# The convolution branch's pointwise projection in three rounded products, beside attention

## The chip, the cores and the metric

The kernel runs on one core of one Trainium2 chip. The metric is the device time of one execution, in microseconds (us), lowest to highest over three runs with their median. Inside a core, TensorE (PE) multiplies matrices, with its weight loads shown apart as PEld; VectorE (DVE), ScalarE (ACT) and GpSimd (POOL) do the elementwise work; SyncE (SP) issues most DMAs. Each engine works through its own instructions in their order and waits for the others on semaphores.

## What is computed

Two transformer-like blocks on 256 tokens of width 1024. The change lies in the first block, in the branch that runs beside attention:

```python
def conformer_conv(u, conv_w, conv_b, ln_g, ln_b, w_pw):
    a, g = jnp.split(u, 2, axis=-1)
    y = a * jax.nn.sigmoid(g)
    y = lax.conv_general_dilated(y, conv_w[:, None, :], ...) + conv_b
    y = jax.nn.silu(layer_norm(y, ln_g, ln_b))
    return y @ w_pw

def merge_branches(u, attn_heads, ...):
    y_a = attn_heads.reshape(b, n, N_HEADS * V_DIM) @ w_o_mla
    y_c = conformer_conv(...)
    g = jax.nn.sigmoid(u[..., OFF_GATE:])
    return (g[..., :D_MODEL] * y_a + g[..., D_MODEL:] * y_c) @ w_out
```

Attention has 16 heads, 256 queries and 512 keys. After it come a retrieval layer that gathers 256 pairs of rows per token lane by index, and a second block with a routed mixture of experts.

## The kernel before

**Layout.** Activations lie with features on the partitions: `convz` is the normed convolution output, [128, 8, 256], eight slices k of 128 features. Weights come through three ring buffers of 2 MB each (`ring`), loaded by SP in the order of `STREAM`; a load waits until `w_used` says that the buffer's former block was taken up.

**Two ways to multiply.** A float32 matmul of 128x256 stands in the trace as two records. Where a product is made "in three", weight and activation are each cut in a rounded high part (type fp32r) and the rest: ACT copies 1024 columns of weights to a `hi` buffer (`weight_round`, L1484; the ACT helper is L1416 in the trace), POOL subtracts it from the ring in place (L1938, the `lo` part), and PE adds hi x hi, hi x lo (L775) and lo x hi (L780), one record each. Before the change this is done for the input projection (28 weight tiles), the attention output projection `w_o` (8 tiles) and `w_out` (6). The weight tiles are numbered in one sequence, c; ACT may round tile c once the rounded products of tile c-3 are issued (`split_done`), since there are three `hi` buffers.

**Attention stage.** 32 units n (16 heads, two halves of the queries). PE's order is written out by `attention_order`: scores S(n+2) (L684), transposes T(n) of unit n's probabilities (L869), after every fourth unit a head pair's output O (L899), and some steps C of the convolution projection (L884). A step C is one output slice m and one input slice k, float32, accumulating in `psY`; there are 64 steps, 6 in unit 0, then one or two a unit. DVE works for unit n: row maximum of S(n) (L2115), bias (L2116), then reciprocal (L2120) and scaling by 1/sum (L2121) of unit n-1, head outputs (L2099, L2100), and after every 16 steps C the gate multiplication (L2108). ACT does exp(n) with its row sum, then the eviction of T(n-1). So T(n) needs L2121 of unit n, which in DVE's queue stands behind the row maximum of S(n+1).

**Just before attention** eight groups q, k, v are projected; DVE evicts q (L2082 to L2087), ACT k and v, and in groups 4 to 7 ACT also applies SiLU to two slices of `convz` each. Then DVE sums the modulation (L2094, L2095). POOL has nothing to do from 183 us until unit 30, where the rounding of `w_o` begins.

Of the kernel before, what the change touches and what calls it, by code (L numbers as in the profile page):

```python
# [20 lines left out]
F32 = mybir.dt.float32  # L21
# [24 lines left out]
SPLIT_IN, SPLIT_O, SPLIT_OUT = 28, 8, 6  # L46
AT_O = SPLIT_IN
# [113 lines left out]
def split_block(c):  # L161

    if c < SPLIT_IN:
        return first_block(2 + 2 * (c // 4)), c % 4
    c -= SPLIT_IN
    for name, n, skip in (("w_o", SPLIT_O, 0), ("w_out", SPLIT_OUT, 2)):
        if c < n:
            return STREAM[name] + (c + skip) // 4, (c + skip) % 4  # L170
        c -= n
# [105 lines left out]
def build(nc, w, out):  # L277
# [3 lines left out]
    with ExitStack() as ctx:  # L281
# [13 lines left out]
        def rounded(*places):  # L295
# [21 lines left out]
        attn_hi, attn_lo, merged_hi, merged_lo = rounded(  # L317
            ("attn_hi", 4096, K, T), ("attn_lo", 6144, K, T), ("merged_hi", 18432, K, T), ("merged_lo", 20480, K, T))
# [54 lines left out]
        convz = ar(12288, K, T)  # L373
        qT, kT, V = ar(14336, HEADS, T), ar(18432, HEADS, 2 * T), ar(26624, 4, D)
# [36 lines left out]
        def split_hi(c):  # L411
            return (hi1_a, hi1_b, hi1_c)[c % 3] if c < SPLIT_IN else top_hi[c % 3]
# [252 lines left out]
        def _(pe):  # L665
# [190 lines left out]
            for kind, n in order:  # L856
# [7 lines left out]
                elif kind == "T":  # L864
                    pe.wait_ge(p_ready, n + 1)
                    if n >= 2:
                        pe.wait_ge(pt_copied, n - 1)
                    for j in range(4):
                        last = nc.tensor.transpose(aux(2 + n % 2)[:, j * P:(j + 1) * P],  # L869
                                                   Pb[:, n % 2, j * P:(j + 1) * P], ident)  # L870
                        if n + j == 0:
                            last.then_inc(w_used, 2)
                    last.then_inc(pt_ready, 1)
                elif kind == "C":


                    m, k = divmod(n, K)
                    if n == 0:
                        pe.wait_ge(conv_out, K)
                        pe.wait_ge(stat_used, STATS.index("var") + 1)  # L880
                    if m >= 4 and m % 2 == 0 and k == 0:
                        pe.wait_ge(conv_gated, m // 2 - 1)
                    wt = use(STREAM["w_pw"] + m // 4) if k == 0 and m % 4 == 0 else wt
                    last = nc.tensor.matmul(aux(m // 2 % 2)[:, (m % 2) * T:(m % 2 + 1) * T],  # L884
                                            wt[:, k * 512 + (m % 4) * P:k * 512 + (m % 4 + 1) * P], convz[:, k, :],
                                            start=(k == 0), stop=(k == K - 1))
                    if m == 4 and k == 0:
                        last.then_inc(w_used, 1)
                    if m % 2 and k == K - 1:
                        last.then_inc(conv_proj, 1)  # L890
                else:

                    ps = tile(ATT[kind, n])
                    pe.wait_ge(tile_free["act"], readers[:TILE["v7"] + 1].count("act"))
                    pe.wait_ge(pt_copied, 4 * n + 4)
                    for j in range(4):
                        for h in (2 * n, 2 * n + 1):
                            lo = VD * (h % 2)
                            last = nc.tensor.matmul(ps[lo:lo + VD, 0:T], V[:, j, h * VD:(h + 1) * VD], PT[:, h % 4, j, :],  # L899
                                                    start=(j == 0), stop=(j == 3))  # L900
                    last.then_inc(tile_ready, 1)
# [210 lines left out]
            def second_pair(i, n):  # L1112

                ps = tile(i)
                if n in (0, 6):
                    pe.wait_ge(h_split, 2 * K)
                    pe.wait_ge(h_hi_ready, 2 * K + (n > 0))
# [288 lines left out]
        def _(act):  # L1406
# [132 lines left out]
            for m in range(8):  # L1539
# [5 lines left out]
                if m == 2:  # L1545
                    root()
                if m >= 4:
                    act.wait_ge(convn_ready, 1)
                    for k in (2 * m - 8, 2 * m - 7):
                        fn(convz[:, k, :], convz[:, k, :], ACT.Silu, scale=vcol("ln_g", k),  # L1550
                           bias=vcol("ln_b", k)).then_inc(conv_out, 1)
            fn(warm, ones[:, 0:1], ACT.Exp)

# [9 lines left out]
            for n in range(n_units + 1):  # L1563
                if n < n_units:
# [7 lines left out]
                    act.sem_inc(tile_free["act"], 1)  # L1572
                if n:
# [328 lines left out]
        def _(pool):  # L1902
# [26 lines left out]
            for c in range(SPLITS):  # L1929
                if c == SPLIT_IN:  # L1930
# [5 lines left out]
                    pool.wait_ge(kr_spread, 2)  # L1936
                pool.wait_ge(u_hi_ready, c + 1)
# [16 lines left out]
            for k in range(K):  # L1954
                pool.wait_ge(h_hi_ready, K + k + 1)
# [12 lines left out]
        def _(dve):  # L1968
# [107 lines left out]

            tab = {lo: rope_tab[lo:lo + 32, :].rearrange("p (a t) -> p a t", a=1).broadcast_to([32, 2, T])
                   for lo in (64, 96)}
            for m in range(8):
# [10 lines left out]
                if m == 3:  # L2090
                    dve.wait_ge(convc_ready, 1)
                    tt(convz, convz, over(rstd(5), K), ALU.mult).then_inc(convn_ready, 1)
            dve.wait_ge(tile_free["act"], readers[:TILE["mod2_3"] + 2].count("act"))
# [18 lines left out]
            for n in range(n_units + 1):  # L2112
                if n < n_units:
                    ps = take(ATT["S", n])
                    seq(nc.vector.tensor_reduce(row_max[:, n:n + 1], ps[:, :], AX.X, ALU.max))  # L2115
                    ts(row_bias[:, n:n + 1], row_max[:, n:n + 1], -ATTN_SCALE, None, ALU.mult).then_inc(nbias, 1)  # L2116
                if n:
# [682 lines left out]
def pack(i):  # L2800
# [21 lines left out]
    for e in range(NEXP):  # L2822
# [17 lines left out]
        "w_pw": cols(a("w_pw")[0]),  # L2840
# [35 lines left out]
```

## Time and profile before

| | |
|---|---|
| median of three runs (lowest, highest) | 1516.78 us (1515.97, 1517.38) |
| the profiled execution: its own time | 1518.48 us |
| its span in the trace | 1516.3 us |
| busy in the span: PE, PEld, DVE, ACT, POOL | 1267.8, 723.6, 876.7, 553.3, 463.0 us |
| mean granted clock of TensorE | 0.885 of full speed |
| attention stage | about 221 to 310 us from the start |
| retrieval stage, gathers by DMA | about 380 to 1045 us |

The trace is of one execution; its span leaves out some 2 us that lie around it in the execution's own time. Busy times of PE are modelled ends of pipelined matmuls: the pitch from one record's start to the next is what a matmul takes of the engine. Line numbers in rows are those of the kernel before.

### The profile page before, as it was taken

The numbers are of one execution on the slowest core, as the hardware profiler recorded it, in microseconds if no ns is written. First come the engines' busy times: TensorE is split into PE (matmuls) and PEld (weight loads), VectorE is DVE, ScalarE is ACT, GpSimd is POOL, SyncE is SP. The second block draws the span as 40 slices with busy tenths as digits, with TensorE's granted clock in tenths as the row PEclk, the third lists the DMA queues.
The fourth block names the chain that finished last, engine by engine and source line by source line (L and its number), as shares of the span: only waits on it lengthen the run. The fifth ranks groups of instructions, "written<-read, shape, count | busy, mean of one in ns | idle before, by whom it ended". The sixth has DMA issues, their size and how long they took to land.

```text
span 1516.3 us, 19635 instructions
## 1 busy us (share of the span) xinstructions
PE 1267.8 (84%) x7450; PEld 723.6 (48%) x7450; DVE 876.7 (58%) x2110; ACT 553.3 (36%) x1107; POOL 463.0 (31%) x374
## 2 busy tenths in 40 slices
PE   7999999999787666666766776677999999999997
PEld 3888766689543111111111312113878987554543
DVE  2799786654598888864555654445647552222112
ACT  2244364532343333332333222224785523212122
POOL 0546600073333333333333332330526413000000
PEclk9999999999999667767677887767999999999999
DMA  9466612145999999999999999999333348899996
GB/s 373 196 254 255 248 66 95 56 177 223 404 370 396 422 415 422 412 421 421 421 421 417 421 421 422 420 421 373 112 111 112 112 183 346 333 428 427 427 427 257
DMA packets 53806, 479.14 MB, mean 316 GB/s; under 512 B 6353, under 2 KB 6737, under 8 KB 8145
## 3 DMA queue, kind: packets, MB, share of 16 engines
q0 software_dynamic: 36864, 268.45, 42.9%
q1 hardware_dynamic: 15552, 206.99, 34.0%
q10 hardware_dynamic: 1296, 2.45, 0.4%
q8 instruction: 59, 0.97, 0.3%
q14 instruction: 35, 0.28, 0.0%
HBM read 476.82 MB, written 1.05 MB: 315 GB/s over the span
## 4 chain that ended last, share of the span: by engine, by line
PE 51%; DMA 29%; DVE 11%; ACT 4%; issue 3%; POOL 1%; SPq 0%; DVEq 0%; ACTq 0%; POOLq 0%
DMA arena<-in_uv,pick 24%; PE psD L684 13%; PE psD L775 7%; PE psD L1303 6%; PE psY L953 5%; DVE arena L2220 5%; PE psD L780 4%; PE psD L1312 3%; ACT arena L1416 3%; DMA arena<-in_experts 2%; PE psY L884 2%; DMA ring<-in_w_in 2%; PE psY L1253 1%; DMA ring<-in_w_mod 1%; PE psY L684 1%
## 5 line engine op out<-in xcount | busy, mean ns | idle before, releaser
L953 PE MATMUL psY<-arena 64*64 64x512 f32 x2048 | 379.4, 835 | 199.9 <-ACT arena L1416 196.1
L1926 POOL DMA_INDIRECT arena<-in_uv,pick x256 | 240.0, 938 | 419.5 <-PE psY L953 400.8
L953 PEld LDWEIGHTS psY<-arena 64*64 64x64 f32 x2048 | 67.7, 163 | 485.4 <-ACT arena L1416 458.2
L2220 DVE CUSTOM_DVE_ANT_0 arena<-arena,psD 128x1024 f32<-128x1024 f32 x128 | 156.3, 1221 | 155.4 <-DMA arena<-in_uv,pick 152.3
L1416 ACT ACTIVATE arena<-arena,pick 128x64 f32<-128x64 f32 x256 | 88.8, 347 | 391.6 <-DVE pick L2220 369.4
L2220 DVE CUSTOM_DVE_ANT_0 arena<-arena,psY 128x1024 f32<-128x1024 f32 x128 | 154.5, 1215 | 56.4 <-DMA arena<-in_uv,pick 55.9
L1416 ACT ACTIVATE arena<-psD 64x512 f32<-64x512 f32 (+4 forms) x128 | 67.5, 533 | 272.8 <-PE psD L1303 105.5
L1416 ACT ACTIVATE arena<-arena 128x64 f32<-128x64 f32 (+4 forms) x301 | 116.3, 387 | 24.5 <-DVE arena L2636 4.6
L2050 DVE SCALAR_TENSOR_TENSOR psY<-arena,pick,psY 128x256 f32<-128x256 f32 x224 | 89.2, 482 | 0.0
L684 PE MATMUL psD<-arena 128*128 128x128 f32 (+3 forms) x420 | 84.5, 345 | 3.7 <-DVEq L2661 2.6
L1416 ACT ACT_TABLE_LOAD x60 | 77.0, 1283 | 8.0 <-DVE pick L2220 5.8
L684 PEld LDWEIGHTS psD<-arena 128*128 128x128 f32 (+2 forms) x420 | 58.4, 202 | 23.0 <-issue 15.3
L2732 DVE TENSOR_TENSOR yrow_lo<-psD,yrow_hi 64x512 fp32r<-64x512 f32 x32 | 22.0, 689 | 70.9 <-ACT yrow_hi L1416 70.4
L1938 POOL TENSOR_TENSOR ring_r<-ring,work_r 128x1024 fp32r<-128x1024 f32 x9 | 22.8, 2546 | 131.1 <-ACT work_r L1416 131.1
L684 PE MATMUL psD<-arena,ring 128*128 128x256 f32 (+1 forms) x240 | 57.5, 395 | 3.3 <-issue 2.7
L1416 ACT ACTIVATE arena<-psY 128x512 f32<-128x512 f32 (+1 forms) x51 | 30.4, 595 | 68.5 <-PE psY L869 35.7
L684 PEld LDWEIGHTS psD<-arena,ring 128*128 128x128 f32 x240 | 45.3, 190 | 12.6 <-issue 5.9
L910 PE MATMUL psD<-xh,ring 128*128 128x256 f32 x192 | 47.2, 392 | 0.0
L910 PEld LDWEIGHTS psD<-xh,ring 128*128 128x128 f32 x192 | 35.5, 193 | 16.2 <-issue 12.2
L2725 DVE SCALAR_TENSOR_TENSOR arena<-psD,arena 64x512 f32<-64x512 f32 x16 | 12.1, 756 | 48.0 <-ACT arena L1416 47.8
L1303 PE MATMUL psD<-arena,xh 128*64 128x512 f32 x160 | 36.5, 594 | 1.1 <-DMA arena<-in_experts 1.1
L1303 PE MATMUL psD<-arena,work 128*64 128x512 f32 x160 | 36.6, 594 | 0.7 <-ACT work L1416 0.7
(441 smaller groups left out, 2373.0 us busy)
## 6 DMA issues: line engine op xcount, KB each, us to landing
arena<-in_experts SPq DMA_DIRECT2D x30, 2048.0 KB, 19.7
ring<-in_w_in SPq DMA_DIRECT2D x18, 2048.0 KB, 9.4
ring<-in_experts SPq DMA_DIRECT2D x18, 2048.0 KB, 17.5
ring<-in_w_mod SPq DMA_DIRECT2D x12, 2048.0 KB, 9.0
ring<-in_w_pq SPq DMA_DIRECT2D x4, 2048.0 KB, 8.2
ring<-in_w_out SPq DMA_DIRECT2D x3, 2048.0 KB, 8.4
ring<-in_w_pw SPq DMA_DIRECT2D x2, 2048.0 KB, 8.2
ring<-in_w_o SPq DMA_DIRECT2D x2, 2048.0 KB, 10.7
```

The source lines that it names most:

```text
L684: last = nc.tensor.matmul(dst, a, b, start=(i == 0), stop=(i == len(pairs) - 1))
L775: last = nc.tensor.matmul(ps, hi[:, k * P:(k + 1) * P], x[:, k, :], start=(k + i == 0), stop=False)
L780: last = nc.tensor.matmul(ps, lo[:, k * P:(k + 1) * P], x_hi[:, k, :], start=False, stop=(k == K - 1))
L884: last = nc.tensor.matmul(aux(m // 2 % 2)[:, (m % 2) * T:(m % 2 + 1) * T], wt[:, k * 512 + (m % 4) * P:k * 512 + (m % 4 + 1) * P], convz[: ...
L910: last = nc.tensor.matmul(ps, wt[:, f * D + k * P:f * D + (k + 1) * P], src[:, k, :], start=(k == 0), stop=(k == K - 1))
L953: last = nc.tensor.matmul(y_of[t][at:at + HALF_P, i * 512:(i + 1) * 512], diag[rows, q % DIAGS, :], seats[q % SEATS][rows, D + c * 512:D + ...
L1303: last = nc.tensor.matmul(psD[bank][lo:lo + 64, :], lhs, wt[:, col:col + 512], start=(k == 0), stop=(k == K - 1))
L1312: last = nc.tensor.matmul(psD[bank][lo:lo + 64, :], hidT[:, f, 64 * side:64 * (side + 1)], wd[:, f * D + 8 * lo:f * D + 8 * lo + 512], sta ...
L1416: return nc.scalar.activation(dst, src, f, **kw)
L1926: nc.gpsimd.indirect_dma_start(seats[q % SEATS], None, w["uv"], bass.IndirectOffsetOnAxis(index[:, q:q + 1], 0)).then_inc(gathered[q % SEA ...
L2050: s[j % 2] = mark(stt(cpart if j == TAPS - 2 else acc, y[:, j:j + T], conv_w[:, m * TAPS + j:m * TAPS + j + 1], acc, ALU.mult, ALU.add))
L2220: nc.vector.tensor_tensor_reduce(u_row, u_row, rows_of[t], 1.0, 0.0, ALU.mult, ALU.add, dots[:, q:q + 1]).then_inc(dot_done, 1)
```

## The change

`w_pw` is packed in tiles as `w_o` is and takes eight numbers in the sequence of rounded weights, 28 to 35, ahead of `w_o`. `convz` gets a rounded copy `convz_hi` (in the place of `hT`) and a rest `convz_lo` in its own place. ACT rounds tile 28 in the q, k, v groups after group 3, tile 29 ahead of unit 0's exponential, and tiles 30 to 35 in units 1, 5, 9, 13, 17 and 21, each between exp(n) and the eviction of T(n-1). DVE makes `convz_hi` in four copies of two slices: after groups 5, 6 and 7 and in unit 0. POOL subtracts tile 28, then the four pairs of slices, then tiles 29 to 35. A step C is three records on PE.

```diff
-SPLIT_IN, SPLIT_O, SPLIT_OUT = 28, 8, 6
-AT_O = SPLIT_IN
+SPLIT_IN, SPLIT_PW, SPLIT_O, SPLIT_OUT = 28, 8, 8, 6
+AT_PW = SPLIT_IN
+AT_O = AT_PW + SPLIT_PW
...
+        convz_hi = xh_r[:, 1]
...
-            return (hi1_a, hi1_b, hi1_c)[c % 3] if c < SPLIT_IN else top_hi[c % 3]
+            return (hi1_a, hi1_b, hi1_c)[c % 3] if c < SPLIT_IN else top_hi[(c - SPLIT_IN) % 3]
...
                     if n == 0:
-                        pe.wait_ge(conv_out, K)
                         pe.wait_ge(stat_used, STATS.index("var") + 1)
+                    if m == 0 and k % 2 == 0:
+                        pe.wait_ge(h_split, K + k // 2 + 1)
+                    if k == 0:
+                        pe.wait_ge(u_hi_ready, AT_PW + m + 1)
+                        pe.wait_ge(u_lo_ready, AT_PW + m + 1)
                     if m >= 4 and m % 2 == 0 and k == 0:
                         pe.wait_ge(conv_gated, m // 2 - 1)
-                    wt = use(STREAM["w_pw"] + m // 4) if k == 0 and m % 4 == 0 else wt
-                    last = nc.tensor.matmul(aux(m // 2 % 2)[:, (m % 2) * T:(m % 2 + 1) * T],
-                                            wt[:, k * 512 + (m % 4) * P:k * 512 + (m % 4 + 1) * P], convz[:, k, :],
-                                            start=(k == 0), stop=(k == K - 1))
-                    if m == 4 and k == 0:
-                        last.then_inc(w_used, 1)
+                    hi, lo = split_hi(AT_PW + m), split_at(ring_r, AT_PW + m)
+                    for i, (wt, x) in enumerate(((hi, convz_hi), (hi, convz_lo), (lo, convz_hi))):
+                        last = nc.tensor.matmul(aux(m // 2 % 2)[:, (m % 2) * T:(m % 2 + 1) * T], wt[:, k * P:(k + 1) * P],
+                                                x[:, k, :], start=(k + i == 0), stop=(k == K - 1 and i == 2))
+                        if m == 4 and k + i == 0:
+                            last.then_inc(w_used, 1)
+                        if k == K - 1 and i == 1:
+                            last.then_inc(split_done, 1)
...
+                if m == 3:
+                    act.wait_ge(rstd_ready, 5)
+                    weight_round(AT_PW)
...
             fn(warm, ones[:, 0:1], ACT.Exp)
+            weight_round(AT_PW + 1)
...
                     act.wait_ge(exp_done, n + 1)
                     act.sem_inc(tile_free["act"], 1)
+                if n % 4 == 1 and n < 4 * (SPLIT_PW - 2):
+                    weight_round(AT_PW + 2 + n // 4)
                 if n:
                     turned(n - 1)
...
+                if c == AT_PW + 1:
+                    for i in range(K // 2):
+                        pool.wait_ge(h_hi_ready, K + i + 1)
+                        nc.gpsimd.tensor_tensor(convz_lo[:, 2 * i:2 * i + 2, :], convz[:, 2 * i:2 * i + 2, :],
+                                                convz_hi[:, 2 * i:2 * i + 2, :].bitcast(F32),
+                                                ALU.subtract).then_inc(h_split, 1)
                 pool.wait_ge(u_hi_ready, c + 1)
...
+            def convz_round(i):
+
+                dve.wait_ge(conv_out, 2 * i + 2)
+                nc.vector.tensor_copy(convz_hi[:, 2 * i:2 * i + 2, :],
+                                      convz[:, 2 * i:2 * i + 2, :]).then_inc(h_hi_ready, 1)
...
+                if m >= 5:
+                    convz_round(m - 5)
...
+                if n == 0:
+                    convz_round(3)
                 if n:
                     i = n - 1
                     dve.wait_ge(exp_done, i + 1)
...
-        "w_pw": cols(a("w_pw")[0]),
+        "w_pw": tiles(a("w_pw")[0]),
```

**ACT, at the start of attention.** `arena,per_row<-psD` is an exponential, `arena<-psY` the eviction of a transposed unit, `work_r<-ring` and `top_hi<-ring` a rounding. Before:

```order
L1416 ACTIVATE warm<-cst 128x1
L1416 ACTIVATE arena,per_row<-psD,per_row 128x512 x2
L1416 ACTIVATE arena<-psY 128x4x128
L1416 ACTIVATE arena,per_row<-psD,per_row 128x512
L1416 ACTIVATE arena<-psY 128x4x128
```

With the change:

```order
L1424 ACTIVATE warm<-cst 128x1
L1424 ACTIVATE work_r<-ring 128x1024
L1424 ACTIVATE arena,per_row<-psD,per_row 128x512 x2
L1424 ACTIVATE top_hi<-ring 128x1024
L1424 ACTIVATE arena<-psY 128x4x128
L1424 ACTIVATE arena,per_row<-psD,per_row 128x512
```

Tile 29's rounding stands ahead of exp(0), tile 30's between exp(1) and the eviction of T(0).

**POOL, from the last tile of the input projection on.** Before:

```order
L1935 COPY arena<-arena 32x16x256 x2
L1938 TENSOR_TENSOR ring_r<-ring,work_r 128x1024
L1938 TENSOR_TENSOR ring_r<-ring,top_hi 128x1024
```

With the change:

```order
L1949 COPY arena<-arena 32x16x256 x2
L1958 TENSOR_TENSOR ring_r<-ring,work_r 128x1024
L1954 TENSOR_TENSOR convz_lo<-arena,xh_r 128x512 x4
L1958 TENSOR_TENSOR ring_r<-ring,work_r 128x1024
L1958 TENSOR_TENSOR ring_r<-ring,top_hi 128x1024
```

Eight subtractions of weights and four of slices come ahead of those of `w_o`, which before were POOL's first work in attention.

**DVE, from the last q group to unit 0's scaling, with the change** (`xh_r<-arena` is a copy of two slices; before, the same rows stand without the two of L2100):

```order
L2113 TENSOR_TENSOR arena<-arena 32x512
L2100 CAST xh_r<-arena 128x512
L2122 TENSOR_REDUCE mod<-per_row 128x32
L2123 TENSOR_TENSOR mod<-mod,vec 128x32
L2143 TENSOR_REDUCE per_row<-psD 128x1
L2144 TENSOR_SCALAR per_row<-per_row 128x1
L2100 CAST xh_r<-arena 128x512
L2143 TENSOR_REDUCE per_row<-psD 128x1
L2144 TENSOR_SCALAR per_row<-per_row 128x1
L2150 RECIPROCAL per_row<-per_row 128x1
L2151 TENSOR_SCALAR arena<-arena,per_row 128x512
```

The third and the fourth copy of slices stand ahead of the modulation sum and of unit 1's row maximum.

## Rows read from the trace of the kernel before

**Rows 1.** Windows: the attention stage; busy us (instructions) of each engine, clock, DMA.

```profile
221.30:309.80 88.50, 84.30 (x444) 55.68 (x442) 53.97 (x148) 45.50 (x101) 6.12 (x3) 1.00 0.19 72
```

**Rows 2.** Chain of waits in attention: start us, us, engine, tile, line.

```profile
240.94 0.65 PE psY L869 x4
...
249.34 0.44 PE psY L869 x4
249.77 0.86 PE psY L884 x4
250.64 0.86 PE psD L684 x2
```

**Rows 3.** Chain of waits behind attention: rounded products of one weight tile.

```profile
312.93 1.92 PE psD L775 x16
314.85 0.96 PE psD L780 x8
```

**Rows 4.** Timeline of DVE and POOL at the end of attention.

```profile
303.95 0.16 DVE L2120 RECIPROCAL per_row<-per_row 128x1 f32<-128x1 f32 x1
304.14 1.20 DVE L2121 TENSOR_SCALAR arena<-arena,per_row 128x512 f32<-128x512 f32 x1
...
302.71 2.35 POOL L1938 TENSOR_TENSOR ring_r<-ring,work_r 128x1024 fp32r<-128x1024 f32 x1 [119.82 <-ACT work_r L1416]
```

**Rows 5.** Timeline of DVE and POOL in the second block, where both work on SBUF.

```profile
1077.93 2.33 DVE L2438 TENSOR_SCALAR lbv<-lbv 128x4 f32<-128x4 f32 x1
...
1077.84 2.39 POOL L1960 TENSOR_TENSOR ring_r<-ring,hi_c 128x1024 fp32r<-128x1024 f32 x1
...
1099.30 0.43 DVE L2493 TENSOR_TENSOR arena<-arena 128x256 f32<-128x256 f32 x1
1099.30 2.69 POOL L1960 TENSOR_TENSOR ring_r<-ring,hi_b 128x1024 fp32r<-128x1024 f32 x1 [2.72 <-ACT hi_b L1416]
```

**Rows 6.** Timeline of DVE before unit 0: modulation sum and first row maximum.

```profile
220.45 0.19 DVE L2095 TENSOR_TENSOR mod<-mod,vec 128x32 f32<-128x32 f32 x1
220.68 0.69 DVE L2115 TENSOR_REDUCE per_row<-psD 128x1 f32<-128x512 f32 x1
```

**Rows 7.** Timeline of POOL: eight subtractions of 256 columns.

```profile
62.98 5.73 POOL L1917 TENSOR_TENSOR h_lo<-xh,h_hi 128x256 fp32r<-128x256 f32 x8 [5.10 <-ACT h_hi L1416]
```

**Rows 8.** Timeline of ACT: the exponentials of units 0 and 1.

```profile
222.27 0.67 ACT L1416 ACTIVATE arena<-psD,per_row 128x512 f32<-128x512 f32 x1
...
223.21 0.69 ACT L1416 ACTIVATE arena<-psD,per_row 128x512 f32<-128x512 f32 x1 [0.18 <-ACT arena L1416]
```

**Rows 9.** Timeline of PE: the transposes of units 0 and 2.

```profile
223.90 0.63 PE L869 MATMUL psY<-cst,arena 128*128 128x128 f32 x4
...
226.95 0.65 PE L869 MATMUL psY<-cst,arena 128*128 128x128 f32 x4
```

**Rows 10.** Timeline of ACT and POOL: a rounding, and the subtraction that waits for it.

```profile
87.86 1.06 ACT L1416 ACTIVATE hi_c<-ring 128x1024 fp32r<-128x1024 f32 x1
...
88.99 2.39 POOL L1938 TENSOR_TENSOR ring_r<-ring,hi_c 128x1024 fp32r<-128x1024 f32 x1 [0.95 <-ACT hi_c L1416]
```

**Rows 11.** Timeline of ACT, DVE, PE, unit 5: exponential (then unit 4's eviction), scaling, transposes.

```profile
230.33 0.69 ACT L1416 ACTIVATE arena<-psD,per_row 128x512 f32<-128x512 f32 x1
...
231.97 0.60 ACT L1416 ACTIVATE arena<-psY 128x512 f32<-128x512 f32 x1 [0.86 <-PE psY L869]
...
232.52 0.49 DVE L2121 TENSOR_SCALAR arena<-arena,per_row 128x512 f32<-128x512 f32 x1
...
233.50 0.60 PE L869 MATMUL psY<-cst,arena 128*128 128x128 f32 x4
```

**Rows 12.** The same of unit 9: exponential and scaling.

```profile
242.12 0.68 ACT L1416 ACTIVATE arena<-psD,per_row 128x512 f32<-128x512 f32 x1
...
244.34 0.49 DVE L2121 TENSOR_SCALAR arena<-arena,per_row 128x512 f32<-128x512 f32 x1
```

**Rows 13.** DMA issues: the blocks of the pointwise weights, KB each, median us to landing.

```profile
ring<-in_w_pw SPq DMA_DIRECT2D x2, 2048.0 KB, 8.2
```

More of the change, by code:

```diff
@@ L167, in split_block @@
     c -= SPLIT_IN
-    for name, n, skip in (("w_o", SPLIT_O, 0), ("w_out", SPLIT_OUT, 2)):
+    for name, n, skip in (("w_pw", SPLIT_PW, 0), ("w_o", SPLIT_O, 0), ("w_out", SPLIT_OUT, 2)):
         if c < n:
@@ L316, in build @@
             ("h1_lo", 4096, K, T), ("h1_hi", 16384, K, T), ("hi1_a", 27648, D), ("hi1_b", 28672, D), ("hi1_c", 29696, D))
-        attn_hi, attn_lo, merged_hi, merged_lo = rounded(
-            ("attn_hi", 4096, K, T), ("attn_lo", 6144, K, T), ("merged_hi", 18432, K, T), ("merged_lo", 20480, K, T))
+        attn_hi, attn_lo, convz_lo, merged_hi, merged_lo = rounded(
+            ("attn_hi", 4096, K, T), ("attn_lo", 6144, K, T), ("convz_lo", 12288, K, T), ("merged_hi", 18432, K, T), ("merged_lo", 20480, K, T))
         hi2_late_b, hi2_late_c, hi2_b, hi2_c, h2_lo, hi2_a = rounded(
@@ L1115, in second_pair @@
                 if n in (0, 6):
-                    pe.wait_ge(h_split, 2 * K)
-                    pe.wait_ge(h_hi_ready, 2 * K + (n > 0))
+                    pe.wait_ge(h_split, 2 * K + K // 2)
+                    pe.wait_ge(h_hi_ready, 2 * K + K // 2 + (n > 0))
                 for j in range(2):
@@ L1954, in _ @@
             for k in range(K):
-                pool.wait_ge(h_hi_ready, K + k + 1)
+                pool.wait_ge(h_hi_ready, K + K // 2 + k + 1)
                 nc.gpsimd.tensor_tensor(h2_lo[:, k, :], hT[:, k, :], h2_hi[:, k, :].bitcast(F32),
```

## Prediction

> **What bounds the kernel now.** I read the windows first. From 221.3 to 309.8 us, the stretch that the change rewrites, PE is busy 84.3 of 88.5 us at full clock; DVE has 54, ACT 45.5, POOL 6.1 [rows 1]. The chain of waits says the same: unit after unit it runs T 0.44, C 0.86, S 0.86 on PE without a gap [rows 2], 2.16 us a unit. It leaves PE at a few places only, such as 240.94, where T waits for DVE's scaling; these are the units behind a gate multiplication. Everything after attention waits for its output, so each us won or lost here moves the end by as much.
>
> **PE's saving.** C's 0.86 are four records, two steps of 0.43. A step becomes three rounded records. Such records are issued every 0.12 us (16 in 1.92, 8 in 0.96 [rows 3]), so a step takes 0.36: 0.07 less, 64 x 0.072 = 4.6 us in all. This is the most that can be won.
>
> **What it costs: POOL beside DVE.** POOL, idle in attention before, now makes eight subtractions of 2.4 us and four of slices; a slice pair lies between 0.72 (5.73/8 [rows 7]) and 2.4, by columns 1.3. One row shows what POOL's subtraction does to L2121, which reads and writes SBUF: normally 0.49 [rows 11], beside the subtraction 1.20, ending 0.28 after POOL's end (304.14 + 1.20 = 305.34 against 302.71 + 2.35 = 305.06) [rows 4]. A DVE operation of four columns took 2.33, started 0.09 after a POOL one and ending with it [rows 5]. The reverse is there too: at 1099.30 both start, DVE takes its usual time and POOL 2.69 in place of 2.4 [rows 5]. So one waits until the other is through; DVE goes first with a difference of 0, POOL with one of 0.09.
>
> *Start of attention.* Tile 28 lies under group 4, and its weights land long before; the second block is issued at unit 0's transposes and lands some 8 us later [rows 13], while tile 32 is wanted in unit 9: no cost. Each slice copy takes DVE about 0.4, and the ones after groups 5 to 7 mostly fill gaps. The third releases POOL's slice subtraction at about 220.9. L2095 (two SBUF inputs, 0.19 [rows 6]) falls beside it and ends at 222.3, so the first row maximum starts at 222.35 and not 220.68, and exp(0) at 223.4. ACT's rounding of tile 29 (1.06 [rows 10], behind 222.27 [rows 8]) gives the same 223.3 by itself: the two overlap. Then each scaling meets a subtraction. Scaling 0, due 224.7, is held by the fourth slice pair until 225.4: T(0) at 225.4, not 223.90. Scaling 1, due 226.3, is held by tile 29 to 228.1; scaling 2, due 229.0, by tile 30 (round done at 226.9, POOL from 227.9 behind tile 29) to 230.8. T(2) is at 230.85, not 226.95 [rows 9]: **+3.9 us**. From T(3) on PE is the bound again.
>
> *Tiles 31 to 35,* in units 5, 9, 13, 17, 21. ACT idles 0.86 before an eviction [rows 11]; the 1.06 of a rounding overhangs by 0.2, and the next exponential has over a us to spare: hidden. POOL starts at exp(n) + 0.94 (the shortest distance from an exponential to what follows, [rows 8]) + 1.13 (rounding's start to POOL's start [rows 10]) = exp(n) + 2.07. The scaling of unit n started at exp(n) + 2.19 in unit 5 [rows 11] (13 and 21 alike) and + 2.22 in unit 9 [rows 12] (17 alike). Two steps C lie in that stretch and shorten it by 0.145: + 2.045 and + 2.075. So DVE is ahead by 0.025 in three units and level in two. By the bounds above (0 goes to DVE, 0.09 to POOL) DVE goes first in all five. POOL then ends near exp(n) + 4.8 and holds the next unit's scaling by half a us, but an output O of 1.9 lies on PE before that unit's transposes: hidden.
>
> *Savings that arrive.* Of the 57 steps behind T(2) 4.1 us; those of units 29 and 30 are lost (T(31) hangs on tile 36's rounding and subtraction, [rows 4], which are as long as before), and three single steps behind gates are covered by DVE: about 0.5. So -3.6.
>
> **Sum.** +3.9 - 3.6 = +0.3 us on a span of 1516.3. Nothing behind attention changes but its start. The profiled execution took 1518.48, the median of runs is 1516.78; on the median the forecast is **1517.1**. Its own range is 1515.5 to 1519: unit-0 estimates are good to a us, and a bias operation of one column (L2116) beside POOL, which no row shows, could be held for up to 2.4 us at the start; it would rather pass, as the one-column reciprocal at 303.95 did [rows 4].
>
> The Trainium skill, page "SBUF — State Buffer", section "SBUF: two separate sides", says that the pair of ports which VectorE and GpSimd share is an exclusive lock: whoever starts first has it for the whole instruction, and the other blocks. The trace agrees with that [rows 4, 5]. Taken by recorded starts, it would give units 9 and 17 to POOL (2.07 against 2.075), and the sum would be that of the first rival.
>
> **Rivals.**
>
> *1. POOL wins in units 9 and 17.* For it: level starts, and my two offsets are good to some 0.03. Unit 9's scaling then ends at exp + 2.07 + 2.40 + 0.28 = 4.75 and T(9) starts at 4.81, not at 2.075 + 0.55 = 2.63; PE has nothing else to do. +2.2 twice: +4.7 in all, 1521.5.
>
> *2. POOL wins in all five: slower.* It takes 0.03 to 0.1 us: rounded records at 0.13 rather than 0.12, a rounding that ACT issues a little sooner. In units 5, 13, 21 T(n) would be at exp + 3.17 - 0.29 = 2.88 [rows 11] and comes at 4.81: +1.9 three times, 5.8. With rival 1's: +10.5, **1527.3**. The point from which it decides is a scaling that starts more than about 0.05 after POOL does. Against it stands the arithmetic above, by a margin smaller than its own error.
>
> *3. The start is cheap, faster.* If the subtractions held DVE only where POOL starts well ahead, or my chain of three held scalings broke at its first link, the start costs just the rounding before exp(0), about 1 us: 1 - 3.6 = -2.6, 1514.2. Against it: the held scaling that was measured is exactly this pair of instructions [rows 4].
>
> *4. The three products are not issued at 0.12.* Between transposes and scores of float32 they might go at the old 0.216: 192 records would take 41.5 in place of 27.6 us, +14 and more, 1531. The order of instructions shows rounded operands in every step, and at 0.12 they were issued for `w_o` [rows 3]; hardly.
>
> **Chances.** Forecast 0.50; rival 1 0.18; rival 2 0.20; rival 3 0.07; rival 4 and others 0.05. The range takes in rival 2 and all but the far end of rival 3, and leaves out a tenth or less at either side: 1514.6 to 1527.4. One measurement of this kernel can tell about 0.2%, 3 us. Faster by more than that: a part of rival 3, 0.06. Slower: rivals 1, 2 and 4 and a slip in the start, 0.42. Within: 0.52.
>
> **What would show it.** Steps C in chunks of six records in 0.72 us. L2151, the scaling in the changed kernel, at about 0.7, 1.8 and 1.8 in units 0 to 2, then short in units 5, 9, 13, 17, 21 and 0.9 to 1.2 in the unit behind each. POOL's tiles 31 to 35 taking 2.7, not 2.4. T(2) near 231, and the first rounded record of `w_o` near 310.1. Were the scaling itself 2.5 us long in units 5 to 21, with PE idle before T for about 2, the rivals 1 or 2 hold and the forecast's ordering of the two starts is wrong. Were no L2151 longer than 0.6, rival 3 holds.

## The result, and the profile after

The changed kernel takes 1524.28 us (median of 10 runs, 1520.88 to 1528.41) against 1519.40 of the kernel before on the same chip (10 runs). The ratio is 1.0038, 95% interval 1.0026 to 1.0050: slower by 5.8 us. Differences are taken from the ratios here and below, since the kernel before has other medians in other sessions (1517.78, 1517.64 and 1517.71). A second session gave 1.0036 (1.0023 to 1.0049). That is inside the forecast's range, but not its likeliest case (+0.3): it is rival 1, plus a fall of TensorE's clock that no part of the forecast had.

The profiled execution took 1524.52 us, its span 1522.7. PE was busy 1259.6 us, 8.2 less than before; POOL 489.4, 26.4 more. The windows of the attention stage, to be laid beside [rows 1] (us, then busy us and records of PE, PEld, DVE, ACT, POOL, then the granted clock, DMA share, GB/s):

```profile
221.30:309.80 88.50, 77.84 (x475) 52.26 (x473) 61.02 (x146) 48.85 (x104) 21.31 (x9) 0.98 0.19 72
```

PE is busy 6.5 us less in this stretch, and yet attention isn't through at its end: T(31) starts at 309.97, where it stood at 305.40 before. PE now idles, DVE and POOL have grown, and the clock is 0.98, where it was 1.00. The chain of waits says where, first at the start (start us, us, engine, tile, line):

```profile
220.05 1.19 DVE mod L2123
221.24 0.02 issue
221.26 0.70 DVE per_row L2143
...
223.37 0.73 DVE arena L2151
...
224.99 1.62 DVE arena L2151
...
227.51 1.62 DVE arena L2151
229.12 0.04 issue
229.17 0.66 PE psY L871 x4
229.82 0.72 PE psY L891 x6
230.54 0.86 PE psD L686 x2
231.40 0.44 PE psY L871 x4
```

The chain of before ran on PE from the scores on; here it runs on DVE until T(2). The sum of the modulation parts takes 1.19 (it was L2095, 0.19 [rows 6]), and three scalings take 0.73, 1.62 and 1.62. From T(2) on PE has a steady unit of T 0.44, C 0.71, S 0.86: 2.01, against 2.16 [rows 2]. POOL's timeline of the same stretch, and up to unit 9:

```profile
219.90 1.28 POOL L1954 TENSOR_TENSOR convz_lo<-arena,xh_r 128x512 fp32r<-128x512 f32 x1 [2.13 <-DVE xh_r L2100]
222.56 1.26 POOL L1954 TENSOR_TENSOR convz_lo<-arena,xh_r 128x512 fp32r<-128x512 f32 x1 [1.38 <-DVE xh_r L2100]
223.78 2.55 POOL L1958 TENSOR_TENSOR ring_r<-ring,work_r 128x1024 fp32r<-128x1024 f32 x1
226.29 2.54 POOL L1958 TENSOR_TENSOR ring_r<-ring,top_hi 128x1024 fp32r<-128x1024 f32 x1
234.49 2.66 POOL L1958 TENSOR_TENSOR ring_r<-ring,work_r 128x1024 fp32r<-128x1024 f32 x1 [5.66 <-ACT work_r L1424]
245.74 2.34 POOL L1958 TENSOR_TENSOR ring_r<-ring,work_r 128x1024 fp32r<-128x1024 f32 x1 [8.59 <-ACT work_r L1424]
```

Each held scaling ends 0.28 after one of these does: 223.78 + 2.55 = 226.33, and the scaling 224.99 + 1.62 = 226.61. The sum L2123, of 32 columns, ends 0.06 after the slices' 219.90 + 1.28 = 221.18. Now DVE's scalings of units 5, 6 and 9, from its timeline:

```profile
234.44 0.49 DVE L2151 TENSOR_SCALAR arena<-arena,per_row 128x512 f32<-128x512 f32 x1
...
236.44 0.99 DVE L2151 TENSOR_SCALAR arena<-arena,per_row 128x512 f32<-128x512 f32 x1
...
245.72 2.64 DVE L2151 TENSOR_SCALAR arena<-arena,per_row 128x512 f32<-128x512 f32 x1
```

In unit 5 DVE is recorded 0.05 ahead (234.44 against 234.49) and goes first: its scaling takes 0.49, and POOL's subtraction 2.66. In unit 9 DVE is recorded 0.02 ahead (245.72 against 245.74), yet POOL goes first: 2.34 there, 2.64 for the scaling. Units 13 and 21 are like 5, unit 17 like 9 (DVE 271.06, POOL 271.07). In a second profile of the same kernel (below) DVE is recorded 0.04 ahead in unit 17 and still waits:

```profile
269.82 2.66 DVE L2151 TENSOR_SCALAR arena<-arena,per_row 128x512 f32<-128x512 f32 x1
...
269.86 2.34 POOL L1958 TENSOR_TENSOR ring_r<-ring,work_r 128x1024 fp32r<-128x1024 f32 x1 [8.97 <-ACT work_r L1424]
```

That profile has leads of 0.07 in units 5, 13 and 21, and DVE goes first there. What follows on PE in unit 9 of the first profile, from its timeline, and the windows there:

```profile
245.33 1.02 PE L686 MATMUL psD<-arena 96*128 96x512 f32 x2
248.42 0.85 PE L871 MATMUL psY<-cst,arena 128*128 128x128 f32 x4 [2.06 <-DVE arena L2151]
249.20 3.39 PE L907 MATMUL psD<-arena 128*64 128x256 f32 x16
```

```profile
247.00:248.00 1.00, 0.00 (x0) 0.00 (x0) 1.00 (x1) 0.00 (x0) 1.00 (x1) 1.00 0.00 0
248.00:249.00 1.00, 0.58 (x4) 0.46 (x4) 0.96 (x3) 0.00 (x0) 0.08 (x1) 0.87 0.00 0
249.00:250.00 1.00, 1.00 (x6) 0.53 (x6) 0.70 (x3) 0.69 (x2) 0.00 (x0) 0.50 0.00 0
...
252.00:253.00 1.00, 1.00 (x10) 0.54 (x7) 0.36 (x1) 0.00 (x0) 0.00 (x0) 0.92 0.00 0
```

PE idles for 2.06, and as it starts again the granted clock goes from 1.00 to 0.50 of full speed (from 2.4 to 1.2 GHz) for some 3 us: O(1), its 16 records, takes 3.3 where 1.88 is usual. T(9) to T(10) is 5.78; behind unit 17, where an equal gap stands without a fall of the clock, T(17) to T(18) is 4.14.

The place from which I count matters. Executions reach attention up to 3 us apart (DVE's first rope copy, the 64x512 copy of group 0, stands at 188.81 in the trace of before and at 187.72 here), so the table counts from that copy, in us:

| | T(2) | T(8) | T(9) | T(10) | T(31) |
|---|---|---|---|---|---|
| before | 38.14 | 54.35 | 56.08 | 60.36 | 116.59 |
| after | 41.45 | 56.82 | 60.70 | 66.48 | 122.25 |

From this the account of T(31), 5.66 later: start +3.31; units 9 and 17, T(8) to T(9) 3.88 against 1.73, so +2.15 twice, 4.3; clock 5.78 - 4.14 = +1.64; and the rest, 5.66 - 3.31 - 4.3 - 1.64 = **-3.6**, the cheaper products.

### The profile page after: what moved, and what is told of

It reads as the page before. It is cut to its first block, busy times and chain, and to the rows that moved or that the text cites. A ratio compares the mean times of both kernels' runs of the same rounds, so it can differ in the third digit from the quotient of the medians.

```text
span 1522.7 us, 19802 instructions
## 1 busy us (share of the span) xinstructions
PE 1259.6 (83%) x7514; PEld 720.8 (47%) x7514; DVE 887.4 (58%) x2114; ACT 561.1 (37%) x1115; POOL 489.4 (32%) x386
## 3 DMA queue, kind: packets, MB, share of 16 engines
HBM read 476.82 MB, written 1.05 MB: 314 GB/s over the span
## 4 chain that ended last, share of the span: by engine, by line
PE 50%; DMA 28%; DVE 14%; ACT 5%; issue 3%; POOL 1%; SPq 0%; DVEq 0%; ACTq 0%; POOLq 0%
DMA arena<-in_uv,pick 23%; PE psD L686 11%; PE psD L777 7%; PE psD L1311 6%; PE psY L961 6%; DVE arena L2250 5%; PE psD L782 4%; PE psD L1320 3%; ACT arena L1424 3%; DMA arena<-in_experts 2%; PE psD L918 2%; DMA ring<-in_w_in 2%; PE psY L1261 1%; DMA ring<-in_w_mod 1%; PE psY L891 1%
## 5 line engine op out<-in xcount | busy, mean ns | idle before, releaser
L1424 ACT ACTIVATE arena<-arena 128x64 f32<-128x64 f32 (+4 forms) x301 | 116.3, 387 | 26.4 <-DMA arena<-in_ctxT 4.5
L1958 POOL TENSOR_TENSOR ring_r<-ring,work_r 128x1024 fp32r<-128x1024 f32 x15 | 39.0, 2607 | 68.0 <-ACT work_r L1424 68.0
```

What stands on the lines that cost most here:

```text
L1424: return nc.scalar.activation(dst, src, f, **kw)
L1958: nc.gpsimd.tensor_tensor(split_at(ring_r, c), split_at(ring, c), split_hi(c).bitcast(F32), ALU.subtract).then_inc(u_lo_ready, 1)
```

## Experiments

Theories. **Exclusion:** POOL's subtraction and DVE's two-input or SBUF-to-SBUF work can't run together, and every us lost comes from DVE held by POOL (with the clock's fall as a consequence of PE's gap). **Rival:** ScalarE's roundings, put between an exponential and a turned copy, are late by themselves, or the products are. Edits are to the changed kernel.

### Five waits: DVE always first

```diff
+                if AT_PW + 3 <= c < AT_O:
+                    pool.wait_ge(p_ready, 4 * (c - AT_PW - 2) + 2)
                 pool.wait_ge(u_hi_ready, c + 1)
```

> GpSimd waits for the scaling of units 5, 9, 13, 17 and 21 before it subtracts tiles 31 to 35; nothing else differs from the changed kernel. Exclusion theory (GpSimd's subtraction and VectorE's scaling can't run together, and GpSimd went first in units 9 and 17): both scalings of 2.64 us become 0.49, T(9) and T(17) come some 2.2 us sooner each, and TensorE's stretch at a granted clock of 0.50 behind T(9) (about 1.6 us) goes with its idle gap; the scaling in the unit behind each stays at 0.9 to 1.2 and is hidden. 6.0 us less than the changed kernel, some 1518.3. Rival (units 9 and 17 were late because ScalarE's rounding stands before the turned copy there, and the long scaling was idle time anyway): T(9) and T(17) stay where they were and the time stays at 1524, within 1 us.

Measured: 1518.44 us, ratio 0.9998 (0.9986 to 1.0009): 0.0040 or 6.1 us less than the changed kernel. The scalings of units 5, 9, 13, 17 and 21 take 0.49, T(8) to T(9) is 1.73 again, and the scalings of the units behind them take 1.2 to 1.6 under the output O. Unit 9:

```profile
247.96 0.49 DVE L2153 TENSOR_SCALAR arena<-arena,per_row 128x512 f32<-128x512 f32 x1
...
248.52 2.37 POOL L1960 TENSOR_TENSOR ring_r<-ring,work_r 128x1024 fp32r<-128x1024 f32 x1 [8.91 <-DVE arena L2153]
```

The roundings on ScalarE stand where they stood, so they cost nothing: the rival falls.

### The same edge, pushed the other way

```diff
+                    if i in (5, 13, 21):
+                        seq(nc.vector.tensor_copy(row_max[:, i:i + 1], row_sum[:, i:i + 1]))
                     ts(Pb[:, i % 2, :], Pb[:, i % 2, :], row_inv[:, i:i + 1], ...)
```

> In units 5, 13 and 21, where VectorE's scaling was recorded 0.05 us before GpSimd's start, a copy of one column (about 0.08 us) is put ahead of the scaling, so that GpSimd is ahead by 0.03. Exclusion theory: the scalings of these three units go from 0.49 to about 2.6, T of each comes 2.2 us later: 6.6 us more than the changed kernel, some 1530.9; with a stretch of low granted clock behind some of the three gaps (1.6 each) up to 1535.7. Rival (a scaling that starts within the first tenth of a microsecond is not held, and units 9 and 17 are late for a cause of their own): 0.25 us more in all, 1524.5.

Measured: 1533.16 us, ratio 1.0101 (1.0082 to 1.0120), 9.6 more than the changed kernel. Unit 5, from the timelines of DVE and POOL:

```profile
235.12 0.15 DVE L2152 COPY per_row<-per_row 128x1 f32<-128x1 f32 x1
235.31 2.48 DVE L2153 TENSOR_SCALAR arena<-arena,per_row 128x512 f32<-128x512 f32 x1
...
235.17 2.34 POOL L1958 TENSOR_TENSOR ring_r<-ring,work_r 128x1024 fp32r<-128x1024 f32 x1 [5.66 <-ACT work_r L1424]
```

The copy was meant to cost 0.08. It moves the scaling's start by 0.19, from exp(5) + 2.04 to + 2.23, so that POOL is 0.14 ahead, and the scaling of 0.49 becomes one of 2.48. All five units now have it: T(31) stands at 129.75 from the first rope copy, 7.5 later than in the changed kernel; T comes 1.9 later in each of the three, 5.7, and there are two stretches of low clock (263 to 267 and 291 to 295, behind T(13) and T(21)) in place of one, 1.8. The times show 9.6, some 2 more than the trace up to T(31), which is within what the two intervals leave open. This is the forecast's second rival, made on purpose.

### Placement in place of waits

```diff
-                if n % 4 == 1 and n < 4 * (SPLIT_PW - 2):
-                    weight_round(AT_PW + 2 + n // 4)
+                if n == 1:
+                    weight_round(AT_PW + 2)
                 if n:
                     turned(n - 1)
+                if n % 4 == 2 and 6 <= n <= 22:
+                    weight_round(AT_PW + 2 + n // 4)
```

> Tiles 31 to 35 are rounded behind the turned copy of units 6, 10, 14, 18 and 22 instead of between exponential and copy of units 5, 9, 13, 17 and 21; no wait is added. GpSimd then subtracts from some 0.5 us after the scaling of that unit to 2 us or more before the next one, which comes 4 to 5.5 us later since a head's output stands between. Exclusion theory: no scaling over 0.5 us from unit 3 on, T(31) as with the added waits (75 us after T(2)), some 6 less than the changed kernel: 0.9998 of the kernel before. Rival (rounding later keeps ScalarE's next exponential or copy waiting, about 1.06 us in each of five units, and TensorE waits for it): up to 5 us more than that, 1.003.

Measured: 1518.80 us, ratio 1.0002 (0.9989 to 1.0015). T(2) to T(31) is 116.30 - 41.44 = 74.86, against 78.45 in the kernel before: 3.59 less. From unit 3 to 30 no scaling is over 0.49. Here POOL and DVE in unit 9 of this kernel: the tile that unit 9 had is subtracted at 249.29, behind the scalings of units 9 and 10.

```profile
246.43 0.49 DVE L2153 TENSOR_SCALAR arena<-arena,per_row 128x512 f32<-128x512 f32 x1
...
248.09 0.49 DVE L2153 TENSOR_SCALAR arena<-arena,per_row 128x512 f32<-128x512 f32 x1
...
249.29 2.37 POOL L1960 TENSOR_TENSOR ring_r<-ring,work_r 128x1024 fp32r<-128x1024 f32 x1 [8.70 <-ACT work_r L1424]
```

The next exponential does come some 0.9 later (unit 7's at 238.04, where unit 6's scaling starts at 237.15), and nobody waits for it.

### No subtractions of weight tiles

```diff
+                if AT_PW <= c < AT_O:
+                    pool.sem_inc(u_lo_ready, 1)
+                    continue
...
-                    hi, lo = split_hi(AT_PW + m), split_at(ring_r, AT_PW + m)
+                    hi, lo = split_hi(AT_PW + m), convz_lo[:, :, :].rearrange("p k t -> p (k t)")
```

> GpSimd does not subtract tiles 28 to 35, and the third product takes its weights from the slices' rounding errors instead (the lo part of w_pw is left out of the result); roundings on ScalarE, casts, GpSimd's four slices and all three products stay. Exclusion theory: the scalings of units 1 and 2 take 0.5 instead of 1.62, those of 9 and 17 0.49 instead of 2.64, units 6, 14 and 22 0.49: 2.2 + 4.4 less, and the low clock behind T(9) with it, some 1.0038 minus 0.0045 to 0.0055: 0.9988 of the kernel before. Rival (ScalarE's roundings between exponential and copy delay the units by themselves): 1.002 or more.

Measured: 1518.66 us, ratio 0.9996 (0.9983 to 1.0009), of a kernel that leaves a part of the product out. That is 0.0008 over what I expected, within the interval. The trace is sharper: T(2) at 39.59 (1.86 sooner than in the changed kernel), T(31) at 114.43 (7.8 sooner), scalings of 0.49 in units 1 to 30. So of the 3.31 at the start 1.86 belong to the subtractions of tiles 29 and 30; 1.45 stay. Of these, 1.05 stand at exp(0) already (34.52 from the first rope copy, 33.47 before): the casts ahead of it, the held sum L2123 and tile 29's rounding. The other 0.4 comes in unit 0, with the fourth cast and a scaling of 0.73, held by the fourth slice pair.

### The order at the start

```diff
-                if m >= 5:
+                if m in (5, 6):
                     convz_round(m - 5)
...
             seq(tt(mod[:, 16:48, 0], mod[:, 16:48, 0], vcol("b_mod", 16, 32), ALU.add))
+            convz_round(2)
...
-            weight_round(AT_PW + 1)
...
+                if n in (1, 3):
+                    weight_round(AT_PW + 1 + n // 2)
...
+                if c in (AT_PW + 1, AT_PW + 2):
+                    pool.wait_ge(p_ready, 2 * (c - AT_PW))
```

> The order at the start of attention alone is changed: the third cast of the convolution's slices goes behind the sum of the modulation parts (L2123), tiles 29 and 30 are rounded in units 1 and 3 instead of before unit 0 and in unit 1, and GpSimd waits for the scaling of units 1 and 3 before it subtracts them. Exclusion theory (the start costs 3.3 us because GpSimd's slices and tiles 29 and 30 hold VectorE's sum and three scalings): the sum takes 0.3 to 0.4 instead of 1.18, the scalings of units 1 and 2 take 0.5 and at most 1.2 instead of 1.62 each, T(2) comes 2.5 to 3.0 sooner; time 2.7 less than the changed kernel, some 1521.6. Rival (the start is bound by ScalarE's exponentials and TensorE's order, and the held scalings lie in their shade): T(2) comes less than 0.8 sooner, 1523.5 or more.

Measured: 1522.53 us, ratio 1.0038 (1.0024 to 1.0052): no difference from the changed kernel. In the trace the sum takes 0.19 and scaling 1 0.49, but scaling 2 takes 1.45, since at this pace (exponentials 1.4 to 2.1 apart) there is no place for 2.4 us of POOL between two scalings. From exp(0) to T(2) it is 6.45, against 6.93. A miss in size: the start can be had back by 1.3, not by 2.5 to 3.

The profile has T(2) at 41.31 all the same, which by itself would be the expectation's rival (under 0.8 sooner). It is the place of counting that misleads here, since the clock is low across the first rope copy, at 186.05:

```profile
185.00:188.00 3.00, 3.00 (x6) 1.65 (x5) 1.90 (x3) 0.24 (x1) 0.00 (x0) 0.50 0.96 300
```

The second rope copy comes 4.65 behind the first, where 3.44 is usual. Counted from the second, T(2) is at 36.66, as in the run below, and at 38.01 in the changed kernel: 1.35 sooner. Behind T(17), from 270 to 273, the clock fell to 0.50 once more.

### Both orders

This has the diff of the five waits and that of the start.

> Both orders together. If the two costs are separate and the cheaper products are worth their 3.6 us: 6.0 + 2.7 less than the changed kernel, some 1515.6, which is 3.8 less than the kernel before (1519.4). Rival (what is taken out at the start comes back as a wait later, since another engine than TensorE bounds attention by then): no less than the better of the two alone, 1518.3.

Measured: 1515.81 us, ratio **0.9986** (0.9974 to 0.9999): faster than the kernel before by 2.1 us, by an interval that just leaves out 1, and 7.6 to 7.9 less than the changed kernel. POOL's timeline at its start:

```profile
222.23 1.27 POOL L1955 TENSOR_TENSOR convz_lo<-arena,xh_r 128x512 fp32r<-128x512 f32 x1 [0.36 <-DVE xh_r L2105]
225.25 2.37 POOL L1963 TENSOR_TENSOR ring_r<-ring,work_r 128x1024 fp32r<-128x1024 f32 x1 [1.74 <-DVE arena L2157]
229.35 2.37 POOL L1963 TENSOR_TENSOR ring_r<-ring,top_hi 128x1024 fp32r<-128x1024 f32 x1 [1.74 <-DVE arena L2157]
```

T(2) is at 40.11 and T(31) at 115.03 from the first rope copy, 1.56 sooner than before, with the clock at 1.00 throughout.

### The start's order with placement

This has the start's diff and the placement's, and no waits for tiles 31 to 35.

> The start's order (tiles 29 and 30 rounded in units 1 and 3 behind the wait for the scaling, the third cast behind the modulation's sum) together with the roundings of tiles 31 to 35 behind the turned copies, without a wait for them. From the first rope copy to T(2) 40.1, T(2) to T(31) 74.9, no scaling over 0.5 from unit 7 on: 1.6 us less than the kernel before in attention, 0.9988. Rival (what attention gains is given back behind it): 1.000.

Measured: 1517.49 us, ratio 0.9993 (0.9981 to 1.0005). T(2) at 40.09, T(31) at 115.00, as the run before to 0.03 us.

### Casts on ScalarE, the sum out of the way

```diff
+                    if m < 7:
+                        act.wait_ge(conv_out, 2 * m - 6)
+                        fn(convz_hi[:, 2 * m - 8:2 * m - 6, :], ..., ACT.Copy).then_inc(h_hi_ready, 1)
...
+                if n == 8:
+                    seq(tt(mod[:, 16:48, 0], mod[:, 16:48, 0], vcol("b_mod", 16, 32), ALU.add))
...
+                    pool.wait_ge(p_ready, c - AT_PW + 2)
...
-    return 6 + (K * K - 6) * n // (HEADS * TT - 1)
+    return 6 + (K * K - 6) * n // (HEADS * TT - 1) - (n == 2)
```

Tiles 29 and 30 are rounded in units 1 and 3, and tiles 31 to 35 are placed as above.

> Roundings placed as in the run before last (behind the turned copies), tile 29 rounded in unit 1 and tile 30 in unit 3 with GpSimd waiting for the scaling of units 2 and 3, slices 0 to 2 cast by ScalarE behind their activations, the sum L2123 put behind the scaling of unit 7, and the first product with tile 29 one unit later. Exclusion theory: from the first rope copy to T(2) 38.3 us (40.1 with both orders, 38.1 before), T(2) to T(31) 75 us: 3.3 us less than the kernel before, 0.998. Rival (ScalarE, with three casts more, becomes late for the first exponential): T(2) at 39.5 or later, 0.9986 as with both orders.

Measured: 1518.06 us, ratio 0.9996 (0.9981 to 1.0010). T(2) came nearly as hoped, at 38.67. But the two tiles now hold the scalings of units 3 and 4 (1.77 and 1.85), where PE is the bound, and T(8) is at 55.46: 16.8 behind T(2) where the others need 15.4. T(31) at 114.96 is where the two runs above have it. The holding moved and cost as much.

### One product less

```diff
-                    for i, (wt, x) in enumerate(((hi, convz_hi), (hi, convz_lo), (lo, convz_hi))):
+                    for i, (wt, x) in enumerate(((hi, convz_hi), (lo, convz_hi))):
...
```

This kernel has the placement of tiles 31 to 35 and the changed kernel's start, and leaves out the product with `convz_lo`.

> As the run with the roundings behind the turned copies, without the product of rounded weights and the slices' rounding errors (that term is left out of the result; GpSimd's four slices are still made). If TensorE's own time bounds attention behind T(2): 57 steps by 0.12 less, T(2) to T(31) 68.0 us instead of 74.9, and 6.8 off the time, 0.9957 of the kernel before. Rival (exponential, scaling and turned copy bound a unit at 2.0 us as they are): less than 2 off, 0.999 or more.

Measured: 1512.75 us, ratio 0.9962 (0.9948 to 0.9975), 0.0040 or 6.1 less than with three products. PE's own time is the bound behind T(2). T(2) to T(31) is 69.31, 5.55 less than 74.86 where 57 x 0.12 = 6.84 was expected. The intervals that did not shrink are those in the shade of DVE: T(8) to T(9) and T(16) to T(17), under a gate multiplication (both 1.73 against 1.72), and the last, where T(31) waits for the scaling that tile 36's subtraction holds (it grows by 0.23). (This profile has a stretch of low clock as well, at 225 to 228 behind T(0), while DVE is the bound.) The chain shows the shade: C, then DVE's multiplication and all that is queued behind it, then T:

```profile
238.60 0.25 PE psY L891 x2
238.85 0.02 issue
238.87 0.69 DVE arena L2138
239.56 0.61 DVE per_row L2145
...
240.45 0.50 DVE arena L2153
240.95 0.04 issue
241.00 0.66 PE psY L871 x4
```

### The clock: the gap filled

```diff
+                    if n in (9, 17):
+                        pe.wait_ge(pt_copied, n - 1)
+                        for _ in range(14):
+                            nc.tensor.transpose(aux(2 + n % 2)[:, 0:P], ident, ident)
                     pe.wait_ge(p_ready, n + 1)
```

> The changed kernel with 14 further transposes of the identity (0.11 us each, 1.5 in all) in front of T(9) and of T(17), into the bank that T overwrites, so that TensorE works through most of the 2.1 us in which it waits for the held scaling. The scalings stay at 2.64. Theory that the idle gap brings the clock down: no stretch of granted clock under 0.9 behind T(9), T(9) to T(10) 4.1 to 4.2 instead of 5.78, time 1.6 less than the changed kernel: 1.0037 minus 0.001. Rival (the stretch has another cause): T(9) to T(10) stays at 5.8 and the time at 1.0037.

Measured: 1524.09 us, ratio **1.0027** (1.0012 to 1.0041), 0.0010 less than the changed kernel, the size expected but with intervals that overlap. So the times don't decide. In the one profile the scaling still takes 2.65, the clock stays at 1.00, and T(9) to T(10) is 4.15. From PE's timeline and the windows:

```profile
246.70 1.69 PE L870 MATMUL psY<-cst 128*128 128x128 f32 x14
248.94 0.66 PE L875 MATMUL psY<-cst,arena 128*128 128x128 f32 x4 [0.55 <-DVE arena L2155]
```

```profile
249.00:250.00 1.00, 1.00 (x8) 0.70 (x10) 0.93 (x4) 0.36 (x1) 0.00 (x0) 1.00 0.00 0
250.00:251.00 1.00, 1.00 (x12) 0.70 (x10) 0.27 (x1) 0.90 (x3) 0.00 (x0) 1.00 0.00 0
```

### Two second profiles

> The changed kernel once more, unedited, for a second profile of it. If the idle gap of TensorE before T(9) itself brings the clock down, the stretch of granted clock 0.50 stands again behind T(9), at O(1), and makes it 3.3 us. If such a stretch comes and goes from one execution to the next, it stands elsewhere or nowhere, while the two scalings of 2.64 us in units 9 and 17 stand as before. Time 1.0038 of the kernel before, as measured.

Measured: 1523.94 us, ratio 1.0036. The low clock stands in the same place (0.50 to 0.77 from 248 to 252), T(9) to T(10) is 5.77, and again there is none behind T(17).

> The kernel with the five waits once more, for a second profile: whether the stretch of low clock at 230 to 234, which no long scaling stands in front of, comes back in the same place (then it belongs to this order of work) or not (then it belongs to the execution).

Measured: 1515.05 us, one run. The first profile of that kernel had four windows at 0.50 to 0.73 from 230 to 234, among units that no held scaling precedes but the start's; the second has 1.00 there, and T(31) at 116.29 against 118.84. Of this 2.55, 1.6 is that stretch (T(2) to T(31) 76.45 against 74.85); the rest is a stretch of low clock across the first rope copy of the first profile, as in the kernel with the start's order. So these stretches come and go from one execution to the next.

## Why the prediction was right, and where it was wrong

The time lies in the recorded range, 1514.6 to 1527.4, because that range took in the slower rivals. The forecast's own case, +0.3 us with a range of its own of 1515.5 to 1519, did not come; +5.8 did. So the mechanism was foreseen, and which of its cases holds was not.

**PE's saving: right.** Six records take 0.71 to 0.72. The saving that arrives was put at 3.6, with the last units and those under gates left out, and is 3.6, both by the account above and by the placement run (3.59).

**The start: right in mechanism, too dear by 0.6.** I had T(2) 3.9 later; it is 3.3. The scalings take 0.73, 1.62, 1.62 for my 0.7, 1.8, 1.8. L2123 ended at 221.24, and at 222.3 in the forecast; all of this difference is that the whole execution was 1.09 sooner at its first rope copy. The 0.6 grows over scalings 1 and 2, which ended 0.4 and 0.6 sooner, counted from there, than I had them.

**Exclusion: right.** Held scalings end 0.28 after POOL, as [rows 4] had it. The one-column operations pass beside it, which the forecast took from the reciprocal at 303.95: L2144 at 223.11 takes 0.15 inside the subtraction of 222.56 to 223.82.

**Units 5, 9, 13, 17, 21: the step that failed.** "By the bounds above (0 goes to DVE, 0.09 to POOL) DVE goes first in all five." The offsets were good: the scaling starts at exp(n) + 2.04 in unit 5 and + 2.06 in unit 9, forecast 2.045 and 2.075; POOL at + 2.09 and + 2.08, forecast 2.07. It was right for 5, 13 and 21, wrong for 9 and 17. Between bounds of 0 and 0.09 I read a difference near 0 as DVE's, from a single row with a level start [rows 5]. That row is of a two-input product of 256 columns, which goes first at a level start in all fourteen profiles of this study; the bound doesn't carry over to the scaling. For it recorded leads of 0.01 to 0.04 were not enough, and leads of 0.05 to 0.07 were. Rival 1's price, 2.2 a unit, was right (2.15). By the exclusive lock of the Trainium skill, page "SBUF — State Buffer", section "SBUF: two separate sides", the text gave these two units to POOL; that came true. Yet the recorded starts of the changed kernel, taken literally, would give them to DVE: the lock is borne out, since one always waits until the other is through, but starts recorded 0.02 apart don't say who was first.

**The clock: missing.** No term of the sum, and no rival, asked what PE's gap does to PE's clock. It is +1.6. Six of the seven stretches at 0.50 in attention, over all profiles, start within 0.9 us of the end of a PE gap of 1.7 to 2.2, and in the fill run, with 0.55 of the gap left, there is none. That speaks for the gap as the cause, from one profile and with gaps that no fall follows, so it isn't proved. Without the fall rival 1's sum would have been met: +3.3 + 4.3 - 3.6 = 4.0 against its 4.7; with it, 5.66 in the trace and 5.8 in the times.

**The chances.** Rival 1 had 0.18 against 0.50 for the forecast, although the text itself said that the offsets were good to 0.03 and the margin was 0 in units 9 and 17. With such a margin the two cases deserved equal chances, and slower than 0.2% more than 0.42. The delayed run shows how near the edge the other three units are as well: 0.19 us more makes it 1533. Two of the rivals' own figures are off besides: rival 3's 1514.2 lies outside the range said to take in all but its far end, and rival 4's 1531 leaves out the start's 3.9. Neither rival came: the records of C stand 0.12 apart, and the start costs 3.3.

**What stays open.** Whether the kernel with both orders beats the one before. Its trace, and those of the two other reordered starts, are 1.6 us shorter up to T(31), each time at the same figure. The measured ratios are 0.9986, 0.9993 and 0.9996, 1.3 us on average, and only the first interval lies below 1. From T(31) to the first gather all fourteen profiles agree (73.8 to 73.9), but to the end of the span they differ by up to 3.7 us (1210.9 before, 1214.0 and 1211.3 in the two profiles of the kernel with five waits): by up to 3.2 up to the last gather's issue and by up to 3.5 behind it, in stages that the change doesn't touch. The 1210.9 of the kernel before is the least of them, from one profile, and may be chance. A gain of 1.6 is at the limit of what can be told. Also open is how the 1.05 up to exp(0) divides among casts, sum and rounding.

## What to carry to other kernels

When work is given to an idle GpSimd beside VectorE operations that it excludes, give it a place, not a chance: look for the stretch in which VectorE waits for something else (here behind a head's output, 4 to 5.5 us), or make it wait until VectorE's short operation is through. An order that rests on a tenth of a microsecond is worth a rival of equal chance. And a gap of 2 us on TensorE may cost more than its length, since the work behind it can run at half the clock.

## What the runs showed of the hardware that I had not expected

- **Recorded starts name the winner only with an offset, and not the same for every operation.** In five profiles the scaling meets GpSimd's subtraction in these units (the changed kernel twice, the start's order, the late scalings, the filled gap). Recorded 0.01 to 0.04 ahead (units 9 and 17), VectorE's scaling was held for 2.1 us, ten times of ten; recorded 0.05 to 0.07 ahead (5, 13, 21) it was not, twelve of twelve, and GpSimd took 2.63 to 2.66 for its 2.4. The short leads stand in the same two units each time, so something else in those units isn't ruled out; the late scalings show that the other three are lost too once GpSimd is ahead.
- **The clock fell behind idle gaps of 1.7 to 2.2 us, though not behind each.** In the fourteen profiles of this study PE has twelve such gaps in attention: two in the changed kernel, in both of its profiles, two with the start's order, five with the late scalings, and one, before T(0), where a product is left out. Six are followed by some 3 us at 0.50 of full speed, which cost about 1.6 where PE is the bound. None follows the 22 gaps of 1.3 to 1.5, or the two filled ones. One further stretch, in the first profile of the kernel with five waits, came behind the start's gaps of 1.47, 0.57 and 0.97. Ahead of the first q, k, v group, where the kernels are alike, PE idles 2.5 to 2.7 us in all fourteen, and in six a stretch at 0.50 begins there, between 0.3 before and 1.3 after the gap's end. In the changed kernel it is the same gap of the two in both profiles, which two profiles can't tell from chance. What picks the gap isn't known. The Trainium skill, page "TensorE: Matmul & The Clock Gate", section "What's actually happening", says that the clock is set by how busy TensorE has been recently; the direction agrees, and no run here shows why one gap of 2.06 counts and the next does not.
- **A late start is bought back only where the pace allows.** At the start, with scalings 1.4 to 2.1 us apart, every place for a subtraction of 2.4 held one of them, whichever place was tried.
